# Hybrid encoder layer on one core: seven more pairs of input tiles by seven-product multiplication, and recurrence heads with carried decays

## The reference, cut to what matters

```python
def rmsnorm(x, gain): return x * rsqrt(mean(x*x, -1) + EPS) * gain
# x (1, 1024, 2048); one layer, all float32
h = rmsnorm(x, norm_gain)
proj = h @ w_in                       # 2048 -> 7552 columns = 59 tiles of 128
aq, af, ai, ag, bq, bk, bv, bg, cq, ck, cv, cg = split(proj)
# A, 6 heads (128x128 state): f = lb + (1-lb)*sigmoid(af); k = 1-f
#   S_t = diag(f_t) S_{t-1} + k_t i_t^T ;  o_t = S_t^T silu(q_t)/sqrt(128); per-head rms
# B, 5 heads: banded softmax attention with a learned clipped relative bias
# C, 5 heads: retention with a fixed decay per head, rotary q and k; per-head rms
y = concat(ya*silu(ag), yb*silu(bg), yc*silu(cg))      # 2048 columns
out = rmsnorm(x + y @ w_out, final_gain)
```

## Time and profile before

| | |
|---|---|
| runs | 1776.45 us median of 3 (1775.53 to 1777.09) |
| the profiled execution | 1775.75 us, of which the span from first to last instruction is 1774.0 us |
| TensorE matmul busy | 1739.8 us, 98% |
| VectorE, ScalarE, GpSimd busy | 1206.9 (68%), 674.6 (38%), 773.4 us (44%) |
| DMA | 323.29 MB, mean 182 GB/s |
| granted TensorE clock, mean | 0.997 |

### The profile page before, as it was taken

The page is one execution under the profiler, slowest core; times in us unless marked ns, Lnnn a source line. Parts: engine busy times, 40 slices in busy tenths (PEclk is TensorE's granted clock), DMA queues, the critical chain, the costliest instruction groups (busy, mean ns, idle before and its releaser), DMA issues.

```text
span 1774.0 us, 26939 instructions
## 1 busy us (share of the span) xinstructions
PE 1739.8 (98%) x10332; PEld 1440.9 (81%) x10332; DVE 1206.9 (68%) x1708; ACT 674.6 (38%) x983; POOL 773.4 (44%) x545
## 2 busy tenths in 40 slices
PE   7999999999999999999999999999999999999996
PEld 5888888888888778888887888888888877888885
DVE  7857665554678988787778356555655458777986
ACT  4423334332435244343443333333544233333442
POOL 4544444444455644444444433333334430354552
PEclk9999999999999999999999999999999999999998
DMA  7768777685888524223323332333433369778876
GB/s 256 233 225 253 244 237 254 220 266 180 299 274 265 161 78 126 90 84 114 96 84 110 119 109 85 97 95 112 144 107 108 91 200 344 253 245 263 280 257 231
DMA packets 160851, 323.29 MB, mean 182 GB/s; under 512 B 18378, under 2 KB 19151, under 8 KB 160724
## 3 DMA queue, kind: packets, MB, share of 16 engines
q1 hardware_dynamic: 146458, 276.52, 49.1%
q10 hardware_dynamic: 14266, 45.05, 7.2%
HBM read 275.35 MB, written 46.15 MB: 181 GB/s over the span
## 4 chain that ended last, share of the span: by engine, by line
PE 95%; DVE 2%; DMA 1%; issue 1%; ACT 0%; POOL 0%; SPq 0%; DVEq 0%; POOLq 0%
PE prj L836 35%; PE prj L815 31%; PE prj L1118 17%; PE mix L981 2%; PE mix L964 2%; PE mix L855 1%; PE mix L974 1%; PE mix L907 1%; DMA in_raw<-in_wi 1%; PE mix L934 1%; PE mix L937 1%; PE mix L923 1%; PE mix L1012 1%; PE mix L1034 1%; PE mix L1023 0%
## 5 line engine op out<-in xcount | busy, mean ns | idle before, releaser
L782 POOL TENSOR_SCALAR w_hi<-w_sum 128x512 fp32r<-128x512 f32 x119 | 193.0, 1622 | 492.8 <-DMA w_sum<-in_w 479.5
L815 PE MATMUL prj<-in_hi,w_hi 128*128 128x512 f32 x840 | 328.7, 391 | 10.9 <-DVE w_lo L1742 9.3
L815 PE MATMUL prj<-in_hi,w_lo 128*128 128x512 f32 x840 | 327.3, 390 | 0.0
L815 PE MATMUL prj<-in_lo,w_hi 128*128 128x512 f32 x840 | 327.3, 390 | 0.0
L836 PE MATMUL prj<-mv_hi,w_hi 128*128 128x512 f32 x928 | 300.0, 404 | 0.9 <-DVE mv_lo L1811 0.9
L768 POOL TENSOR_TENSOR w_sum<-in_raw,in_raw 128x512 f32<-128x512 f32 x150 | 200.1, 1334 | 212.4 <-PE prj L815 202.1
L836 PE MATMUL prj<-mv_lo,w_hi 128*128 128x512 f32 x928 | 287.2, 391 | 0.0
L836 PE MATMUL prj<-mv_hi,w_lo 128*128 128x512 f32 x928 | 286.2, 390 | 0.0
L836 PEld LDWEIGHTS prj<-mv_lo,w_hi 128*128 128x128 f32 x928 | 174.2, 188 | 38.0
L836 PEld LDWEIGHTS prj<-mv_hi,w_lo 128*128 128x128 f32 x928 | 174.2, 188 | 37.9
L815 PEld LDWEIGHTS prj<-in_hi,w_hi 128*128 128x128 f32 x840 | 158.1, 188 | 45.4 <-issue 9.8
(11 more groups left out here) (185 smaller groups left out, 2481.4 us busy)
## 6 DMA issues: line engine op xcount, KB each, us to landing
in_raw<-in_wi SPq DMA_DIRECT2D x360, 256.0 KB, 3.3
raws<-in_wo SPq DMA_DIRECT2D x184, 256.0 KB, 3.8
w_sum<-in_w SPq DMA_DIRECT2D x116, 256.0 KB, 3.0
arena<-z_scratch ACTq DMA_DIRECT2D x56, 512.0 KB, 4.0
y_in<-y_scratch SPq DMA_DIRECT2D x80, 256.0 KB, 4.7
z_scratch<-acc_in SPq DMA_DIRECT2D x60, 256.0 KB, 3.8
z_scratch<-stage SPq DMA_DIRECT2D x26, 512.0 KB, 4.3
x_even<-in_xT SPq DMA_DIRECT2D x44, 256.0 KB, 4.0
```

The costliest lines, as they stand in the source:

```text
L782: nc.gpsimd.tensor_scalar(w_hi[q][:], w_sum[q][:], 1.0, None, ALU.mult).then_inc(w_hi_done, 1)
L815: last = nc.tensor.matmul(out, wt[wslot(n)][:, i % GRAN, :], mv[j % 2][:, i, :], start=(i == 0 and wt is w_hi and mv is in_hi), stop=(i == ...
```

## The change

- `MID_PAIRS = 7`: 14 of the 29 plain tiles become seven further pairs, made by the same seven products in 49 more steps (98 slots) between the input pairs and the 15 plain tiles that stay. The slots go from 232 to 218.
- While the input pairs run, each set of x is also stored to DRAM when it is ready (`store_set`, 112 DMAs of 256 KB). For the second batch the sets are loaded again into the rows of mv_hi and mv_lo (`load_set`, 112 DMAs), and the products read them there (`mid_product`). h itself is therefore made later, in slots 88 to 103 (`H_DUE`), and the first plain tile takes its row blocks in the order `FIRST_ORDER`.
- The weights of the second batch: GpSimd adds the blocks and also makes w_lo; ScalarE makes w_hi. VectorE adds 49 steps into accumulators; the 1/rms factor is not applied to them there, but where the tiles are used.
- The A heads: in place of logs, differences and an exponent per level, the products of f over 2, 4, ... 128 frames are formed (`total_of`, seven steps of halving size), and q and k are carried up from level to level in place (`lv_next`: two half-size products per level). Level 1 is an ordinary level. After the last level, k and q are also the operands of state and output. The three 1024-column products, the scan and the `near_*` steps are gone.
- Slots: A heads 17 apart (`A_AT`), B heads from 111, C heads 8 apart.

```diff
-STD = TO - IN_TILES
+MID_PAIRS = 7
+STD0 = IN_TILES + 2 * MID_PAIRS
+MID_STEPS = 7 * MID_PAIRS
+MID_SLOTS = 2 * MID_STEPS
+STD = TO - STD0
-A_FROM, A_EACH, B_FROM, B_EACH = -4, 20, 121, 12
-C_AT = [183, 192, 201, 210]
+A_AT = [-2, 15, 32, 49, 66, 83]
+LEVEL_AT = [8, 9, 10, 11, 12, 14, 15]
+LEVEL_AT_LAST = [8, 9, 11, 12, 14, 15, 17]
+B_FROM, B_EACH = 111, 12
+C_AT = [173, 181, 189, 197]
+FIRST_ORDER = [1, 2, 0, 3]
-LEVELS = [64, 32, 16, 8, 4, 2, 1]
+LEVELS = [1, 2, 4, 8, 16, 32, 64]
+        H_DUE = [88, 89, 90, 91, 91, 93, 95, 97, 100, 100, 101, 101, 101, 102, 103, 103]
...
+            def store_set(j, i):
+                sp.wait_ge(in_comb_lo, HK * j + (i + 1 if j > 0 else HK))
+                for n, mv in enumerate((in_hi, in_lo)):
+                    sp.dma_start(comb_dram[j, i, n], mv[j % 2][:, i, :].bitcast(F32)).then_inc(comb_out[j % 2], 16)
+            def load_set(j, i):
+                sp.wait_ge(comb_out[j % 2], 256 * (j // 2 + 1))
...
+                for n, mv in enumerate((mv_hi, mv_lo)):
+                    sp.dma_start(slot(mv, j, i).bitcast(F32), comb_dram[j, i, n]).then_inc(set_in[j % 2], 16)
...
+                for j in range(2, 7):
+                    set_at.setdefault(IN_STEPS + MID_PAIRS * (j - 1) + 3 + i // 2, []).append((j, i))
...
-            for n in range(IN_ONE, IN_GRANULES):
-                m = in_raw_of[n][0]
+            for n in range(IN_ONE, ALL_GRANULES):
+                if IN_GRANULES <= n + 1 < ALL_GRANULES and in_two(n + 1):
+                    in_weight_sum(n + 1)
+                src = w_sum[wslot(n)][:] if in_two(n) else in_raw_buf(in_raw_of[n][0])
                 pool.wait_ge(in_w_hi, n + 1)
-                nc.gpsimd.tensor_tensor(w_lo[wslot(n)][:], in_raw_buf(m), w_hi[wslot(n)][:].bitcast(F32),
+                nc.gpsimd.tensor_tensor(w_lo[wslot(n)][:], src, w_hi[wslot(n)][:].bitcast(F32),
...
+            def mid_product(n, rows):
...
+                pe.wait_ge(w_split, n + 1)
+                pe.wait_ge(set_in[j % 2], 256 * (j // 2 + 1))
+                for i in rows:
+                    for wt, mv in ((w_hi, mv_hi), (w_hi, mv_lo), (w_lo, mv_hi)):
+                        last = nc.tensor.matmul(
+                            out, wt[wslot(n)][:, i % GRAN, :], slot(mv, j, i),
...
+            for st in range(IN_STEPS, ALL_STEPS):
+                pe.wait_ge(in_acc_done, st - 3)
+                for q in range(2):
+                    mid_product(2 * st + q, range(GRAN * q, GRAN * q + GRAN))
+                    stages[2 * (st - IN_STEPS) + q]()
...
+            def total_of(u, n):
...
+                halves = totals(n - 1).rearrange("p (a h) -> p a h", h=2)
+                tt(totals(n), halves[:, :, 0], halves[:, :, 1], ALU.mult).then_inc(total_ready, 1)
+            def lv_first(u):
...
+                tt(arr(QE), arr(Q), arr(LV0), ALU.mult).then_inc(lv_ready, 1)
+            def lv_next(u, n):
+                m, size = n % 2, LEVELS[n]
+                dve.wait_ge(filled[m], (A_M0 * u + 1 + n // 2) if m == 0 else (A_M1 * u + 2 + n // 2))
+                dve.wait_ge(total_ready, NL * u + max(n, 1))
...
+                tt(q[:, :, 1, :], q[:, :, 1, :], total[:, :, 0:1].to_broadcast(across), ALU.mult)
+                tt(k[:, :, 0, :], k[:, :, 0, :], total[:, :, 1:2].to_broadcast(across),
                    ALU.mult).then_inc(lv_ready, 1)
```

More of the change, by code:

```diff
@@ L478, in build @@
                 spills += [(v, p, C11), (v, p, C21)]
+        mid_spills = []
+        for v in range(IN_STEPS, ALL_STEPS):
+            j, p = in_at(v)
+            if j == 5:
+                mid_spills += [(v, p, C12), (v, p, C22)]
+            if j == 6:
+                mid_spills += [(v, p, C11), (v, p, C21)]
         def spill_sem(p, c):
@@ L1048, in ones_product @@
                 pe.wait_ge(in_sq_added, sum_done[n] + 1)
-                nc.tensor.matmul(mix[1][:, half(n)], ones[:].bitcast(F32), stage[:, half(1)], start=True,
+                nc.tensor.matmul(mix[1][:, half(n)], ones[:].bitcast(F32), rstd[:, half(1)], start=True,
                                  stop=True).then_inc(ss_ready, 1)
@@ L1062, in _ @@
                     ones_product(0)
-            stages = [nothing] * (2 * NG * STD)
+            stages = [nothing] * SLOTS
             def put(slot, *parts):
@@ L1462, in _ @@
             b_high(0)
+            until(MID_SLOTS + 2 * NG)
             norm_second(A_HEADS)
@@ L1950, in a_query, with until @@
             def a_query(u):
                 silu_finish(2 * u, Q, A_DK ** -0.5, Q)
[L1953 to L1960 removed]
+            due = {"step": IN_STEPS, "row": 0}
+            def until(slot):
+                while due["step"] < ALL_STEPS and 2 * (due["step"] - IN_STEPS) + 2 <= slot:
+                    in_accumulate(due["step"])
+                    due["step"] += 1
+                while due["row"] < KB and H_DUE[due["row"]] <= slot:
+                    h_low(due["row"])
+                    due["row"] += 1
```

595 lines of the change are left out of this document (288 added, 307 removed).

## The result

The changed kernel takes 1800.44 us (median of 4 runs, 1797.69 to 1801.37), the kernel before 1776.77 us beside it: ratio 1.0131, 95% interval 1.0119 to 1.0143. It is slower by 1.3%. The forecast of 1748 us had the sign wrong, and the range ended at 1765.

A forecast was written before the change was run, and what follows sets the result against it. TensorE's in-order matmul queue was taken as the bound (95% of the span). 1775.75 - 38.1 - 3.1 + 2.6 + 2.9 + 1.5 + 3 + 3 = 1747.6, as a median 1748 us; range 1740 to 1765.

The forecast's parts named there:

- point 8: Rows of h beside the last head: 6 us of VectorE work over, +3 us on TensorE (0 to 8).
- point 7: VectorE and GpSimd colliding in SBUF beside A heads: +4 us VectorE per head, +3 us in all on TensorE (0 to 12).
- Points 1, 3, 11: In order: 168 matmuls saved, -38.1 us; one more level without near step, +2.6 us; c_state's weight load 128 columns wide, 0.
- Point 2: TensorE's waits beside head 0 go, as rows of h move away and VectorE's work there halves: -3.1 us.
- Point 4: C heads 8 slots apart: three wait 0.95 us each for a PSUM bank (+2.9 us), the last waits +1.5 us.
- Point 5: VectorE beside the A heads: 47.4 us of work in a 60.8 us head, 78%, so no bound by itself.
- slower rival: VectorE and GpSimd block each other, TensorE stands in the level stages: 1776 to 1828 us, chance 0.07.
- theory A: From the experiments' forecasts: VectorE's and GpSimd's SBUF work add up, about 29 and 43 us in a head.
- Point 9: ScalarE loses eight exponents a head, gains 17 w_hi, and does not hold w_hi back: 0.
- Point 10: DMA and SyncE's queue: storing and loading sets costs 0, at most 4 us for each of five sets.

The follow-up runs named there:

- copies on ScalarE: Kernel of the rows run, with ScalarE instead of VectorE copying levels 5 and 6 out of PSUM: 1771.33 us, ratio 0.9969.
- old kernel doubled: Kernel before the change, with one more GpSimd multiplication per granule of the plain tiles beside its six heads: 1802.72 us, ratio 1.0136.
- hand-over: Changed kernel with VectorE's clamp earlier, its accumulates reordered, and SyncE's weight loads for the first plain tile ahead of stores: 1792.90 us, ratio 1.0087.
- rows run: Changed kernel with low parts, hand-over and next head's forget-gate log reordered, plus x rows 0 to 3 and fourth weights loaded before last stores: 1774.25 us.

## Why the prediction was wrong

The sum on the profiled execution should have been 1747.6 us. The stretch between the input pairs and the output should have taken 830.4 us and took 880.5: 50 us. Heads 1 to 3 are 3 x 10.1 = 30 of them. The last head is two slots longer than the others, 60.8 + 5.4 = 66.2 us and 69.2 with point 8's 3 us; it took 87.56, 18 more. The step that failed is point 7, what VectorE and GpSimd do to each other: it put +4 us on VectorE and +0.7 us on TensorE's path in a head, and the runs show 14 and 10.

- *Points 1, 3, 11, right.* The matmuls went as counted: head 4 is 60.85 us for 60.8. c_state's weight loads take 0.19 us in place of 0.14, and its matmuls start 0.11 us apart in both kernels. *Point 2* held for its own cause, but head 0 has new waits.
- *Point 4, right.* Three transposes wait for L2068, 0.93 us each (0.95 forecast), the last C head 1.8 us (1.5 forecast).
- *Point 5, about right in size.* Its sum was 47.4 us with the collisions of today's GpSimd share, and head 4, where GpSimd is busy for 41% of the time, has 50.9. That this is also the 51 us of point 7 is luck: those were meant for a GpSimd at near 80%. The totals were put at 2.5 us and are about 4 there, and 6 in heads 1 to 3. The error is in its last sentence, "no bound by itself": it set busy time against the head's length. In its in-order queue VectorE also has to wait, for states, levels and ScalarE's results: 8 to 11 us in each of heads 1 to 3, and still 4.5 us (64.66 - 60.15, the second head with copies on ScalarE) where it waits least. So I estimate the room at some 5 us, not the 9.8 between 51 and 60.8.
- *Point 7, the step that failed.* The excess over 0.68 us was taken from 0.14 to 0.25 us, by GpSimd's share. In heads 1 to 3 the level products average 1.46 and 1.16 us, an excess of 0.78 and 0.48, and longer operations up to 1.0 more. VectorE is busy for 61 us a head, 14 over the 47.4 of point 5, not 4; and 10 us come on TensorE's path, not 0.7. Of those 10, TensorE's waits are 7 to 9 us, and in heads 2 and 3 another 1.6 us is the clock, which the forecast left out. The rival that used this mechanism set its turning point at 1.4 us in the mean; it was passed at 1.3, since, as I read it, that rival too counted VectorE's queue as able to fill a head to the end. It also looked for the waits at the levels, where they are 10.2 us; 16.5 are at the sum of squares. It got a chance of 0.07.
- *The slower rival, dismissed wrongly.* I had argued that the old means, none above 1.05 us, speak against it; but those were taken with GpSimd at 44%, and the change was just that. In the runs each held the other up (L1999 of VectorE took 2.13 us for 1.23, GpSimd's operation ahead of it 2.1 for 1.27), and GpSimd's operations alone moved heads of the changed kernel by 8 to 11 us. But that the 29 and 43 us a head of theory A, together 72, come so near to the 70.7 to 71.0 measured is luck. The 29 us in them are the 35 operations of point 7 at 0.82 us, a mean that has collisions in it already. The trace has 30 operations with two SBUF inputs in a head, some 22 us if each takes the shortest time seen for its shape, and GpSimd's 34 at 1.27 us are 43: an estimate of 65 us, for heads of 71. In the old kernel doubled the same estimate is 33 + 40 = 73 us, for heads of 70.8 to 71.9 that hold other work too, and in head 2 of the changed kernel one or the other of the two kinds ran in only 60.6 of its 70.96 us. So the times do not simply add, and with the orders mended and the copies on ScalarE the same operations fit into 63.4 to 66.7 us. The order and the gaps decide how much of the added time shows.
- *Point 8, right place, wrong size.* Orders of queues did more here than VectorE's 6 us of overload: the hand-over and rows runs took 5.1 and 8.4 us out of the last head. Of its 87.56 us 5.3 are half clock behind two waits. What is left in the rows run, 71.87 against 66.2, is of the size of that overload, which no run takes away.
- *Point 9, wrong at the last head.* ScalarE did hold w_hi back, behind a clamp of VectorE's, for 11.46 us.
- *Point 10, right on DMA, wrong on SyncE.* 411.21 MB at 229 GB/s (411 and 235 forecast), and TensorE waited for none of the transfers that the change added. "SyncE holds no weight load behind that wait" speaks of the set loads only; the stores at the end of the batch do hold two back.

## What to carry to other kernels

Before moving work on to GpSimd beside a busy VectorE, add GpSimd's time to VectorE's for operations whose inputs are all in SBUF, each as it is alone, and compare with the stage. The estimates above count those with two inputs; one with a single input, L1987, also took 1.67 us in place of 0.69 when it began inside an operation of GpSimd's. By these estimates that was 65 us for a stage of 60.8 and 73 for one of 68.5, and both got longer; 44 for 60.8 (head 4) and 61 for 68.5 (the old kernel) fitted. It says whether, not by how much. A mean taken with GpSimd half idle says little of it full: 0.82 us for the four level groups before, 1.31 for the level products in heads 1 to 3. Then ask for slack in the in-order queue, its gaps included, not for busy share: 51 of 61 us was already nearly full here. Where a stage ends, read every queue for loads of the next stage that stand behind stores of this one; two such changes were worth 7.5 us (with one of VectorE's order) and 6.2 us here, for a few lines.
